# Expert-up tiles inside the gate-matrix stage, later key products and a final norm by token half, in a fused two-block kernel

## The chip, the cores and the metric

One Trainium2 chip, one core of it. The metric is the device time of one execution in microseconds (us): the median of three runs of the kernel before is 1892.19 us (1892.02 to 1892.68).

## The reference, cut to what matters

Two transformer blocks over 256 tokens of width 1024, one after the other, then a final RMS norm, all in float32. The parts that the change touches are these:

```
# first block, gated delta rule, both directions, 4 heads of 128
A     = where(strict, (k*beta) @ k.T * decay, 0);  t_inv = inverse(A + eye)
W, U  = t_inv @ (k*beta*exp(G)), t_inv @ (v*beta);  state and output by scan
# first block, expert layer (16384 experts, 8 heads, the best 16 of each head per token)
act   = gelu(einsum('td,thkd->thk', h2, u_table[experts]))
y     = einsum('thk,thkd->td', gate * act, v_table[experts])
# second block, feed-forward
u     = causal_dwconv(h @ ffn_up, w, b);  x = x + (gelu(u_gate) * u_val) @ ffn_down
return rms_norm(x, final_norm_g)
```

## The kernel before, in words

Activations lie transposed (features on the partitions, 256 tokens along the free axis). Weights come as one stream of tiles of 128x1024 float32 (512 KB) through a ring of four slots, loaded by SP in order; a slot is loaded again when its tile has been used (`tiles_done`, or `w_lo` where the tile is split). Each engine's program is written out by hand in order; semaphores tie them together.

**Split products.** Most weight tiles are cut into a high part (ScalarE copies to `fp32r`, L1330, L1311) and a low part (VectorE or GpSimd subtracts, L2085, L2008, L2494, L2339). A product is then three `fp32r` passes in place of one float32 product (`PASSES`, L151): an up tile (`experts_up`, L816) is 24 matmuls of 256 columns, a down tile (`experts_down`, L827) 12 of 512. Plain float32 products with whole tiles exist too: `full` (L756) does one tile as 8 products of 256 columns; the trace shows each float32 product as two matmul instructions.

**The expert layer.** There is no gather: all 16384 experts are computed, 128 tiles up and 128 down, and the result is weighted by a gate matrix that is zero but for the chosen ones. `NU` = 48 up tiles run first, while VectorE routes (top 16 of 16); their gelu goes to `Wa` (L1345). Then the gate stage (L851 to L861): for each of 32 groups of 8 tokens, VectorE builds one-hot matrices `hot1` (L2069, L2074) and `hot2` (L2071), ScalarE scales seven slices of `hot1` (L1362), TensorE does 8 float32 products of 128 columns (L860) into one of three pairs of PSUM banks, ScalarE takes the columns from `NU` on out to `Wb` (L1357) and VectorE multiplies the first `NU` into `Wa` (`w_gate`, L2064, behind `hot2` of two groups later). Then 48 down tiles with what is in `Wa` (L864 to L868), and then 80 pairs of one up and one down tile (L869 to L876), each up tile's gelu being gated with `Wb` (L1392, L2101).

**The delta rule.** Four steps `n`; in each, six levels `l` of a blockwise inverse for both directions `d`. Per level TensorE does `level_products` (L595: products, then a transpose of `z`), VectorE masks the products (L1903), TensorE does `level_update` (L612), VectorE subtracts (L1910). Other work is laid between: `tok_turn` (L553, transposes of keys and values by token, moved out by ScalarE at L1240), `key_products` of the next step (L572, behind `level_update` of level 2, waiting on `gaps` that VectorE writes in `gap_rows`, L1818), POOL's products, and on VectorE `mod_tail` (L1809), 32 row sums over 1024 columns of streamed tiles: four before the levels, one or two behind each level. `in_tile(38)` is the last input projection.

**The end.** `ffn_up` and `ffn_down` (L1022, L1040) over 22 blocks; per block ScalarE and VectorE norm, convolve, gate and split the activations. The last `ffn_down` waits for all of it for all 256 tokens; then ScalarE squares the four PSUM banks (L1619), VectorE adds the sums, ScalarE takes the root (L1621), VectorE scales the four banks (L2427), and SP writes them out.

## Time and profile before

| | |
|---|---|
| runs | 1892.02, 1892.19, 1892.68 us |
| profiled execution | 1892.63 us |
| its span, first to last instruction | 1890.6 us |
| mean granted TensorE clock | 0.986 |
| busy share: TensorE, VectorE, ScalarE, GpSimd | 96%, 66%, 53%, 8% |
| delta-rule stage | about 250 to 437 us |
| gate stage | about 682 to 778 us |
| 48 down tiles; 80 up/down pairs | 778 to 911 us; 911 to 1360 us |
| end, from the last `ffn_down` on | 1878 to 1890.6 us |

Times are microseconds from the start of the span unless marked ns. A busy share is an average over stages with different limits. Instructions are named by the line of the kernel that issues them. Idle time of TensorE is named with the instruction that ended it.

### The profile page before, as it was taken

The numbers are of one execution on the slowest core, as the hardware profiler recorded it, in microseconds if no ns is written. First come the engines' busy times: TensorE is split into PE (matmuls) and PEld (weight loads), VectorE is DVE, ScalarE is ACT, GpSimd is POOL, SyncE is SP. The second block draws the span as 40 slices with busy tenths as digits, with TensorE's granted clock in tenths as the row PEclk, the third lists the DMA queues.
The fourth block names the chain that finished last, engine by engine and source line by source line (L and its number), as shares of the span: only waits on it lengthen the run. The fifth ranks groups of instructions, "written<-read, shape, count | busy, mean of one in ns | idle before, by whom it ended". The sixth has DMA issues, their size and how long they took to land.

```text
span 1890.6 us, 34445 instructions
## 1 busy us (share of the span) xinstructions
PE 1806.4 (96%) x11798; PEld 1620.1 (86%) x11798; DVE 1248.8 (66%) x2494; ACT 1005.2 (53%) x2017; POOL 148.9 (8%) x118
## 2 busy tenths in 40 slices
PE   8999999999999977899999999999899999999997
PEld 2878789898899976788899999999799899889997
DVE  2786465565388979766666666666676766348886
ACT  2545633241146679766555555555557667036665
POOL 0000003330164520000000000000000000000000
PEclk9999989899999999999999999999999999999999
DMA  7523232123455520255555555555454533445553
GB/s 265 192 100 106 85 111 76 62 91 133 143 172 176 177 89 1 73 194 191 193 183 188 188 187 187 182 188 187 145 183 145 175 123 123 150 162 179 188 181 119
DMA packets 77267, 283.28 MB, mean 150 GB/s; under 512 B 8576, under 2 KB 8576, under 8 KB 76928
## 3 DMA queue, kind: packets, MB, share of 16 engines
q1 hardware_dynamic: 77184, 282.16, 44.6%
q8 instruction: 53, 0.87, 0.2%
q14 instruction: 30, 0.25, 0.0%
HBM read 281.08 MB, written 1.05 MB: 149 GB/s over the span
## 4 chain that ended last, share of the span: by engine, by line
PE 83%; DVE 11%; ACT 3%; issue 1%; DMA 1%; POOL 1%; PEld 0%; PEldq 0%; POOLq 0%; SPq 0%; DVEq 0%; ACTq 0%
PE banks L834 19%; PE banks L822 17%; PE banks L433 7%; PE banks L1035 7%; PE banks L896 6%; PE banks L763 5%; PE banks L1047 3%; PE banks L620 2%; PE banks L604 2%; DVE split L2071 2%; DVE arena L2069 2%; PE banks L1008 1%; PE banks L786 1%; PE banks L401 1%; PE banks L609 1%
## 5 line engine op out<-in xcount | busy, mean ns | idle before, releaser
L1330 ACT ACTIVATE split<-arena 128x512 fp32r<-128x512 f32 x508 | 318.9, 629 | 146.7 <-PE banks L822 83.3
L822 PEld LDWEIGHTS banks<-split 128*128 128x128 f32 x3072 | 379.5, 192 | 11.1 <-DVE split L2008 3.1
L822 PE MATMUL banks<-split 128*128 128x256 f32 x3072 | 383.0, 283 | 3.2 <-DVE split L2008 2.3
L834 PE MATMUL banks<-split 128*128 128x512 f32 x1536 | 364.9, 391 | 2.7 <-issue 2.7
L2085 DVE TENSOR_TENSOR split<-arena,split 128x512 fp32r<-128x512 f32 x412 | 281.9, 690 | 117.0 <-ACT split L1330 111.3
L834 PEld LDWEIGHTS banks<-split 128*128 128x128 f32 x1536 | 284.3, 189 | 58.8 <-issue 2.9
L1311 ACT ACTIVATE split<-arena 128x512 fp32r<-128x512 f32 x264 | 164.5, 627 | 106.2 <-PE banks L1035 52.1
L896 PE MATMUL banks<-split 128*128 128x256 f32 x1344 | 169.5, 286 | 4.0 <-DVE split L2160 3.9
L896 PEld LDWEIGHTS banks<-split 128*128 128x128 f32 x1344 | 164.7, 193 | 7.6 <-issue 6.6
L433 PEld LDWEIGHTS banks<-split 128*128 128x128 f32 (+1 forms) x936 | 132.0, 191 | 28.2 <-issue 13.9
L433 PE MATMUL banks<-split 128*128 128x256 f32 (+2 forms) x936 | 150.9, 320 | 4.3 <-DVE split L1652 3.4
L1035 PEld LDWEIGHTS banks<-split 128*128 128x128 f32 x1056 | 129.7, 192 | 1.7
L2137 DVE TENSOR_TENSOR split<-arena,split 128x512 fp32r<-128x512 f32 x128 | 87.3, 690 | 65.8 <-ACT split L1311 64.7
L1035 PE MATMUL banks<-split 128*128 128x256 f32 x1056 | 130.8, 283 | 0.0
L2339 DVE TENSOR_TENSOR split<-arena,split 128x512 fp32r<-128x512 f32 x132 | 89.1, 687 | 14.7 <-ACT split L1311 14.6
L2494 POOL TENSOR_TENSOR split<-arena,split 128x512 fp32r<-128x512 f32 x68 | 90.9, 1364 | 71.8 <-DVE split L2008 51.2
L860 PE MATMUL banks<-split,arena 128*128 128x128 f32 x512 | 66.9, 286 | 28.4 <-DVE arena L2074 28.4
L860 PEld LDWEIGHTS banks<-split,arena 128*128 128x128 f32 x512 | 61.9, 198 | 33.4 <-DVE split L2071 29.3
L763 PE MATMUL banks<-arena 128*128 128x256 f32 x384 | 86.4, 385 | 3.7 <-DVE arena L2334 2.2
L763 PEld LDWEIGHTS banks<-arena 128*128 128x128 f32 x384 | 74.0, 193 | 14.8 <-DVE arena L2334 2.6
L1652 DVE TENSOR_TENSOR split<-arena,split 128x512 fp32r<-128x512 f32 x78 | 52.8, 688 | 43.2 <-ACT split L1096 42.4
L2101 DVE TENSOR_TENSOR arena<-arena 128x256 f32<-128x256 f32 x80 | 49.1, 614 | 45.0 <-ACT arena L1392 44.9
(378 smaller groups left out, 2382.5 us busy)
## 6 DMA issues: line engine op xcount, KB each, us to landing
arena<-wstream SPq DMA_DIRECT2D x525, 512.0 KB, 3.3
arena<-x_t SPq DMA_DIRECT2D x1, 2048.0 KB, 12.9
arena<-matsa SPq DMA_DIRECT2D x1, 1234.0 KB, 6.2
out_t<-arena SPq DMA_DIRECT2D x4, 256.0 KB, 2.1
arena<-mats SPq DMA_DIRECT2D x1, 576.0 KB, 7.9
arena<-crow SPq DMA_DIRECT2D x1, 512.0 KB, 7.0
arena<-rows SPq DMA_DIRECT2D x1, 512.0 KB, 5.6
arena<-mats SPq DMA_DIRECT2D x1, 449.0 KB, 3.9
```

The lines of the kernel that those rows point to most:

```text
L433: mm = pe.matmul(ps[0:rows, b, 0:m], w_parts[:, c, (2 * t + k // 4) % 4, P * (k % 4):P * (k % 4) + rows], hp[:, e, k, 0:m], start=(k == 0 ...
L763: mm = pe.matmul(ps[:, b, 0:S], w[:, P * k:P * k + P], src[:, k, :], start=(k == 0), stop=(k == KT - 1))
L822: mm = pe.matmul(ps[:, 4 + b, 0:S], w_parts[:, c, (2 * m + half) % 4, P * k:P * k + P], h_parts[:, e, 4 * half + k, :], start=(half == 0 a ...
L834: mm = pe.matmul(ps[:, 2 * tt + half, :], g_parts[:, e, j % 2, P * tt:P * tt + P], w_parts[:, c, (2 * m + half) % 4, :], start=(first and ...
L860: pe.matmul(ps[:, W_BANKS[g % 3] + t // 4, P * (t % 4):P * (t % 4) + P], hot1[g % 2][:, t, :], hot2[:, g % 2, t, :].bitcast(F32), start=Tr ...
L896: mm = pe.matmul(out, w_parts[:, c, (2 * m + half) % 4, P * k:P * k + P], src[:, e, 4 * half + k, :], start=(half == 0 and k == 0 and c + ...
L1035: mm = pe.matmul(ps[:, 4 + 2 * (f % 2) + m, 0:S], w_parts[:, c, (2 * (M_FFN + x) + half) % 4, P * k:P * k + P], h_parts[:, e, 4 * half + k ...
L1311: act.activation(w_parts[:, 0, h % 4, :], ring[:, slot, 512 * half:512 * half + 512], ACT.Copy).then_inc(sem["w_hi"], 1)
L1330: act.activation(w_parts[:, 0, (2 * m + half) % 4, :], ring[:, peer_slot(m), 512 * half:512 * half + 512], ACT.Copy).then_inc(sem["w_hi"], 1)
L2085: dve.tensor_tensor(w_parts[:, 1, (2 * m + half) % 4, :], ring[:, slot, 512 * half:512 * half + 512], w_parts[:, 0, (2 * m + half) % 4, :] ...
L2339: dve.tensor_tensor(w_parts[:, 1, h % 4, :], ring[:, tile_of(M_FFN + x) % RING, 512 * half:512 * half + 512], w_parts[:, 0, h % 4, :].bitc ...
L2494: pool.tensor_tensor(w_parts[:, 1, (2 * m + half) % 4, :], ring[:, (N_PEER + m) % RING, 512 * half:512 * half + 512], w_parts[:, 0, (2 * m ...
```

## The change

Eight of the up tiles (48 to 55) are no longer split: as float32 tiles they come in another order of the stream (by chunk of 128 features, each tile holding one chunk for all eight) and are multiplied by `h2` as 64 plain products of 256 columns, accumulated in banks 4 to 7: 8 before the gate stage's first group, 52 spread over the groups (one or two ahead of each), 4 behind the last. The gate stage keeps two pairs of banks in place of three, and `w_gate` stands between `hot1` and `hot2`. Chunks 0 to 3 of `h2` stay in a buffer of their own; VectorE rebuilds chunks 4 to 7 there from the high and low parts. The eight tiles' gelu and gating ride in the down loop, which now runs over 56 tiles; 72 pairs follow.

In the delta rule, four of the eight `tok_turn` go around `in_tile(38)`, the others to levels 2 and 4; `key_products` of the next step go ahead of `level_update` of level 3; the `mod_tail` are spread anew. At the end the last convolution, gate, split, down product, squares, root and scaling go by half of the tokens, and the square root's table is called for ahead.

```diff
+NX = 8
+NT = NU + NX
-        W_BANKS = (0, 2, 6)
+        w_banks = lambda g: ps[:, 2 * (g % 2):2 * (g % 2) + 2, :].rearrange("p b (t j) -> p (b t) j", j=P)
+        plain_out = lambda q: ps[:, 4 + q // 2, S * (q % 2):S * (q % 2) + S]
+        plain_done = lambda g: NX + 52 * g // (S // 8 - 1)
...
+            def plain_products(a, b):
+                for k, q in (divmod(c, NX) for c in range(a, b)):
+                    n = N_PEER + NU + 2 + k
+                    if q == 0:
+                        tile_ready(n)
+                        if k >= 4:
+                            pe.wait_ge(sem["normed"], k - 2)
+                    mm = pe.matmul(plain_out(q), tile_at(n)[:, P * q:P * q + P], h2k[:, k % 4, :], start=(k == 0 and q % 2 == 0),
+                                   stop=(k == KT - 1), skip_group_check=True)
+                    if q % 4 == 3:
+                        mm.then_inc(sem["tiles_done" if q == 7 else "half_used"], 1)
+            plain_products(0, plain_done(0))
             for g in range(S // 8):
+                if g:
+                    plain_products(plain_done(g - 1), plain_done(g))
                 pe.wait_ge(sem["hot2_ready"], g + 1)
-                if g >= 3:
-                    pe.wait_ge(sem["w_gated"], g - 2)
+                if g >= 2:
+                    pe.wait_ge(sem["w_gated"], g - 1)
...
+            plain_products(plain_done(S // 8 - 1), NX * KT)
# ScalarE, down loop
+            def expert_gelu(j, i=0):
+                if j < NT:
+                    out = plain_out(j - NU)
...
+                if j + 2 < NU:
                     done_hi(j + 2, i, step)
-                peer_hi(NU + j + 2, 1, i, step // 4)
+                elif j + 2 < NT:
+                    gated_hi(j + 2)
+                peer_hi(NT + j + 2, 1, i, step // 4)
+                if NU <= j + 4 < NT:
+                    expert_gelu(j + 4)
# VectorE, gate stage
+            def plain_used(k):
+                dve.wait_ge(sem["tiles_done"], N_PEER + NU + k + 1)
+                dve.sem_inc(sem["w_lo"], 2)
+                if k < 4:
+                    dve.tensor_tensor(h2k[:, k, :], h_parts[:, 0, 4 + k, :].bitcast(F32), h_parts[:, 1, 4 + k, :].bitcast(F32),
+                                      ALU.add).then_inc(sem["normed"], 1)
...
+                if g >= 2:
+                    w_gate(g - 2)
                 dve.tensor_tensor(hot2[:, g % 2, :, :], ...).then_inc(sem["hot2_ready"], 1)
...
-                if g >= 2:
-                    w_gate(g - 2)
+                for k in range(KT):
+                    if g >= 2 and plain_done(g - 3 if g > 2 else -99) < NX * (k + 1) <= plain_done(g - 2):
+                        plain_used(k)
# delta rule, TensorE
             key_products(0, 1)
+            tok_turn(0)
+            tok_turn(1)
             in_tile(38)
+            tok_turn(2)
+            tok_turn(3)
...
-                    if n == 0 and l < 5:
-                        tok_turn(2 * l - 2)
-                        tok_turn(2 * l - 1)
+                    if n == 0 and l in (2, 4):
+                        tok_turn(2 + l)
+                        tok_turn(3 + l)
...
+                    if n < 3 and l == 3:
+                        for d in range(2):
+                            key_products(n + 1, d)
                     for d in range(2):
                         level_update(n, l, d)
...
-                            if l == 2:
-                                key_products(n + 1, d)
# delta rule, VectorE
-            for q in range(2):
-                mod_tail(next(tails))
+            TAILS = ((2, 1, 1, 1, 2, 3), (1, 0, 1, 0, 2, 2), (1, 1, 0, 0, 2, 2), (1, 1, 1, 1, 2, 2))
-                    for q in range(2 if (n, l) in ((0, 1), (0, 2), (3, 4), (3, 5)) else 1):
+                    for q in range(TAILS[n][l - 1]):
                         mod_tail(next(tails))
# the end, TensorE
+            def last_down():
+                f, x = FT - 1, 3 * FT - 1
+                for tt in range(2):
+                    pe.wait_ge(sem["g_lo"], P + f + tt + 1)
+                    for half in range(2):
+                        pe.wait_ge(sem["w_lo"], 2 * (M_FFN + x) + half + 1)
+                        for c, e in PASSES:
+                            mm = pe.matmul(ps[:, 2 * tt + half, :], ...)
+                        mm.then_inc(sem["bank_final"], 1)
# the end, ScalarE
+            last_parts()
+            act.activation(small[:, 84:85], eps, ACT.Sqrt)
...
+            for tt in range(2):
+                final_square(2 * tt)
+                link(final_square(2 * tt + 1))
+                final_root(tt)
# the end, VectorE
+            last_taps(0)
+            last_gate(0)
+            last_taps(1)
+            last_gate(1)
+            for tt in range(2):
+                last_lo(tt)
+            for tt in range(2):
+                dve.wait_ge(sem["final_root"], tt + 1)
+                link(dve.reciprocal(vec[:, 62 + tt:63 + tt], vec[:, 60 + tt:61 + tt]))
+                for b in range(2 * tt, 2 * tt + 2):
+                    dve.scalar_tensor_tensor(outb[:, b, :], ps[:, b, :], vec[:, 62 + tt:63 + tt], ...)
```

## Rows read from the trace of the kernel before

**Rows 1.** The page: shares of the chain that ended last, by engine and line.
```profile
PE 83%; DVE 11%; ACT 3%; issue 1%; DMA 1%; POOL 1%; PEld 0%; PEldq 0%; POOLq 0%; SPq 0%; DVEq 0%; ACTq 0%
PE banks L834 19%; PE banks L822 17%; PE banks L433 7%; PE banks L1035 7%; PE banks L896 6%; PE banks L763 5%; PE banks L1047 3%; PE banks L620 2%; PE banks L604 2%; DVE split L2071 2%; DVE arena L2069 2%; PE banks L1008 1%; PE banks L786 1%; PE banks L401 1%; PE banks L609 1%
```
**Rows 2.** The chain in time, down loop and pairs: start us, length us, what.
```profile
778.38 132.31 PE banks L834 x576
...
941.67 2.87 PE banks L822 x24
944.54 2.75 PE banks L834 x12
```
**Rows 3.** The chain in time, eight plain float32 tiles.
```profile
468.55 27.89 PE banks L763 x128
```
**Rows 4.** The chain in time, gate stage: first group, one middle group, last group.
```profile
684.31 3.77 PE banks L860 x16
...
719.64 1.00 DVE arena L2069
720.64 1.14 DVE split L2071
721.77 0.26 DVE arena L2074
722.03 0.47 DVE arena L2064
...
773.63 2.04 PE banks L860 x16
```
**Rows 5.** Timeline, a middle group: start, us, engine, line, instruction, [idle before].
```profile
722.17 2.02 PE L860 MATMUL banks<-split,arena 128*128 128x128 f32 x16 [0.84 <-DVE arena L2074]
...
723.53 2.16 ACT L1362 ACTIVATE arena<-arena 128x128 f32<-128x128 f32 x7
```
**Rows 6.** Windows: us, then busy of PE, PEld, DVE, ACT, POOL, clock, DMA, GB/s.
```profile
259.00:274.20 15.20, 15.18 (x108) 14.97 (x108) 8.57 (x17) 4.56 (x8) 0.82 (x1) 0.78 0.49 166
684.30:690.00 5.70, 5.69 (x29) 5.70 (x30) 4.16 (x5) 4.35 (x14) 0.00 (x0) 0.56 0.00 1
703.00:740.00 37.00, 26.13 (x209) 24.04 (x208) 37.00 (x53) 35.49 (x105) 0.00 (x0) 1.00 0.01 1
```
**Rows 7.** The chain in time, delta rule: level 1 products and a full-clock x16 group.
```profile
262.44 1.60 PE banks L604 x8
...
269.03 0.84 PE banks L604 x8
...
328.03 1.79 PE banks L584 x16
```
**Rows 8.** Timeline, delta rule: key products with the idle before them, one tail.
```profile
275.78 3.31 PE L577 MATMUL banks<-arena 128*128 128x128 f32 x16 [1.57 <-DVE arena L1823]
...
317.35 3.64 PE L577 MATMUL banks<-arena 128*128 128x128 f32 x16 [2.04 <-DVE arena L1826]
...
318.73 1.22 DVE L1813 SCALAR_TENSOR_TENSOR arena<-arena 128x1024 f32<-128x1024 f32 x1
...
362.41 3.78 PE L577 MATMUL banks<-arena 128*128 128x128 f32 x16 [2.04 <-DVE arena L1826]
```
**Rows 9.** Waits, delta rule, 249.8 to 440: who for whom, total us, times, longest.
```profile
PE banks L620 <- DVE arena L1903: 3.4, 5, 1.4
```
**Rows 10.** The chain in time, the end.
```profile
1878.05 3.04 PE banks L1047 x12
...
1881.10 2.42 ACT arena L1619 x8
...
1883.55 1.28 ACT L1621
1884.83 0.32 ACTq L78
...
1885.37 0.75 DVE arena L2427
```

More of the change, by code:

```diff
@@ L235, in build @@
         rT = top("rT", 3, S)
+        h2k = top("h2k", 4, S)
         h2T = buf("h2T", KT, S)
+        h2 = lambda k, n=1: (h2k if k < 4 else h2T)[:, k % 4:k % 4 + n, :]
         yT = buf("yT", KT, S)
@@ L605, in level_products @@
                 mm.then_inc(sem["y_done"], 1)
-                if l == 1 and n:
-                    pe.wait_ge(sem["wu_ready"], step_at(n - 1, d))
+                if l == 1:
+                    if n:
+                        pe.wait_ge(sem["wu_ready"], step_at(n - 1, d))
+                    else:
+                        pe.wait_ge(sem["tok_ready"], 3 + d)
                 for h in range(4):
@@ L1047, in ffn_down @@
                             mm = pe.matmul(ps[:, 2 * tt + half, :], g_parts[:, e, f % 2, P * tt:P * tt + P],
-                                           w_parts[:, c, (2 * (M_FFN + x) + half) % 4, :], start=False, stop=(last and c == 1),
+                                           w_parts[:, c, (2 * (M_FFN + x) + half) % 4, :], start=False, stop=False,
                                            skip_group_check=True)
@@ L1370, in done_hi, with gated_hi, down_step @@
                     sem["g_hi"], 1)
[L1372 to L1379 removed]
+            def expert_gelu(j, i=0):
+                if j < NT:
+                    out = plain_out(j - NU)
+                else:
+                    used(2 * j - 1 if j > NT else 2 * NT, 1, i, 4)
+                    out = ps[:, 4 + j % 2, 0:S]
+                act.activation(gelu[:, j % 2, :], out, ACT.Gelu_apprx_tanh).then_inc(sem["gelu_done"], 1)
+            def gated_hi(j, i=0):
+                act.wait_ge(sem["gated"], 2 * i + j - NU + 1)
+                act.activation(g_parts[:, 0, j % 2, :], gated[:, j % 2, :], ACT.Copy).then_inc(sem["g_hi"], 1)
+            def down_step(j, i=0, step=0):
+                used(NT + j, 0, i, step)
+                peer_hi(NT + j + 2, 0, i, step // 4)
+                used(NT + j, 1, i, step)
+                if j + 2 < NU:
+                    done_hi(j + 2, i, step)
+                elif j + 2 < NT:
[3 more added lines that the diff above has]
+                    expert_gelu(j + 4)
             act.wait_ge(sem["w_gated"], S // 8)
@@ L1386, in _ @@
                     down_step(j, i, 4)
-            for j in range(NU - 4, NU):
-                down_step(j, last=(j >= NU - 2))
-            def expert_gelu(j, i=0):
-                used(2 * j - 1 if j > NU else 2 * NU, 1, i, 4)
-                act.activation(gelu[:, j % 2, :], ps[:, 4 + j % 2, 0:S], ACT.Gelu_apprx_tanh).then_inc(sem["gelu_done"], 1)
-            def gated_hi(j, i=0):
-                act.wait_ge(sem["gated"], 2 * i + j - NU + 1)
-                act.activation(g_parts[:, 0, j % 2, :], gated[:, j % 2, :], ACT.Copy).then_inc(sem["g_hi"], 1)
+            for j in range(NU - 4, NT):
+                down_step(j)
             def step(j, i=0, last=False):
@@ L1593, in ff_step @@
                 ahead(x + 1, 1, i4)
-                up_out(f, 1, i4)
-                ff_gelu(f, i4)
-                used(x + 2, 0, i4)
-                ahead(x + 2, 0, i4)
-                used(x + 2, 1, i4)
-                ahead(x + 2, 1, i4)
+                if f < FT - 1:
+                    up_out(f, 1, i4)
+                    ff_gelu(f, i4)
+                else:
+                    ff_gelu(f)
+                    last_up_out()
+                if f < FT - 1:
+                    used(x + 2, 0, i4)
+                    ahead(x + 2, 0, i4)
+                    used(x + 2, 1, i4)
+                    ahead(x + 2, 1, i4)
             for x in range(2):
@@ L2091, in done_lo @@
                                   g_parts[:, 0, j % 2, :].bitcast(F32), ALU.subtract).then_inc(sem["g_lo"], 1)
-            def down_step(j, i=0, step=0, last=False):
-                tile_lo(NU + j + 2, 0, i, step // 4)
-                if not last:
-                    done_lo(j + 2, i, step)
-                tile_lo(NU + j + 2, 1, i, step // 4)
             def gate(j, i=0):
@@ L2107, in gated_lo, with down_step @@
                     sem["g_lo"], 1)
+            def down_step(j, i=0, step=0):
+                tile_lo(NT + j + 2, 0, i, step // 4)
+                if j + 2 < NU:
+                    done_lo(j + 2, i, step)
+                elif j + 2 < NT:
+                    gated_lo(j + 2)
+                tile_lo(NT + j + 2, 1, i, step // 4)
+                if NU <= j + 3 < NT:
+                    gate(j + 3)
             def step(j, i=0, last=False):
@@ L2122, in _ @@
                     down_step(j, i, 4)
-            for j in range(NU - 4, NU):
-                down_step(j, last=(j >= NU - 2))
-            tile_lo(2 * NU + 2, 0)
-            gate(NU)
-            gated_lo(NU)
-            with dve.Fori(0, (P - 2 - NU) // 2) as i:
-                for j in (NU + 1, NU + 2):
+            for j in range(NU - 4, NT):
+                down_step(j)
+            tile_lo(2 * NT + 2, 0)
+            gate(NT)
+            gated_lo(NT)
+            with dve.Fori(0, (P - 2 - NT) // 2) as i:
+                for j in (NT + 1, NT + 2):
                     step(j, i)
```

145 lines of the change are left out of this document (90 added, 55 removed).

## The prediction

> **What bounds the kernel now.** I read the page's chain first: TensorE holds 83% of the path that ended last, VectorE 11%, ScalarE 3% [rows 1]. So most of the time is a row of matmuls, and what a removed matmul is worth depends on whether its stage is in the 83 or in the 11. The chain in order of time tells that. In the expert layer's down loop and pair loop nothing but TensorE stands in it: 48 down tiles in 132.3 us, that is 2.76 each, and each up tile 2.87 [rows 2]. In the gate stage it is the reverse: the middle group is VectorE from end to end, 1.00 + 1.14 + 0.26 + 0.47 = 2.87 us per group of 8 tokens [rows 4], and TensorE works 2.02 of it and then idles 0.84 [rows 5]. The windows say the same of 703 to 740 us: VectorE busy 37.00 of 37.00, ScalarE 35.49, TensorE 26.13 at full clock [rows 6]. Thus a down or up tile costs its full price, and TensorE work of up to 0.84 us per group should be free. In the delta rule I read the timeline for idle in front of `key_products` [rows 8] and the waits for VectorE's masks [rows 9]; at the end of the kernel everything is serial [rows 10].
>
> **Part by part.** The sum is made against the profiled execution, 1892.63 us (span 1890.6 and 2.0 around it), 0.44 above the median.
>
> *1. Eight up tiles leave the pair loop.* 8 x 2.87 [rows 2] = -23.0. The down tiles stay 128 in number. Eight down steps get a gelu and a gating beside them; TensorE's 2.76 per step covers them, since ScalarE and VectorE do the same gelu and gating beside two tiles' splits in the pair loop without appearing in its chain. Splits of these eight tiles fall away too, at no gain, being hidden already. Should the cover fail, eight steps would each lose some tenths: 0 to +4, taken 0.
>
> *2. The plain products.* A whole tile of 8 such products took 27.89 / 8 = 3.49 us, or 0.436 each [rows 3]; 64 take 27.9. Of these 52 lie over 31 groups: 21 groups get two, 10 get one. A group is then 2.02 + 0.87 = 2.89 or 2.02 + 0.44 = 2.46 on TensorE, on average 2.75, against VectorE's 2.87: it fits with 0.12 to spare, and a group of two runs over by 0.02, given back by the next of one. VectorE asks for TensorE's results only two groups later, so this overrun reaches nobody. Price 0.
>
> The 8 products ahead of the first group do lie on the path. VectorE's first three instructions (1.00 + 1.14 + 0.26 with starts) end just before the first product at 684.31 [rows 4], so the stage opens some 2.6 us earlier, at 681.7. At full clock 8 x 0.436 = 3.5 end at 685.2, 0.9 late; but then the first group, which now takes 3.77 at half clock, would take 2.04 [rows 4]: -0.8 in all. At half clock, which stood after this same gap (0.56 granted in 684 to 690 [rows 6]), they take 7.0, to 688.7: +4.4. The third `hot1` waits for that group. I take +1.5.
>
> The last 4 products, 1.7 us, run while ScalarE takes out and VectorE gates the last group. Price 0. The tiles come by DMA in a stage that moves almost nothing (0.01 DMA share [rows 6]); the first four slots are free as early as now.
>
> *3. VectorE and the order in the gate stage.* Four sums of 256 columns that rebuild `h2`; the trace's 384-column operation takes 0.47 [rows 4], so 0 to +1.9, taken +1.4. On VectorE each is ahead of the next `hot1`. `w_gate` ahead of `hot2` costs nothing itself, but it now wants ScalarE's copy of two groups before right after `hot1`. ScalarE needs 2.16 for seven slices [rows 5] and the copy behind them; at 35.49 of 37.00 busy [rows 6] its copy ends just about when `hot1` does. Queued behind that wait are `hot2`, the last slice and the next `hot1`. A lag of 0 to 0.1 in 31 groups is 0 to +3; I take +0.5. The third pair of banks is not missed: with two, TensorE waits for a gate that now comes 1.4 us earlier in VectorE's order.
>
> Gate stage together: 1.5 + 1.4 + 0.5 = +3.4 (from -0.8 to +9.3).
>
> *4. Delta rule, key products.* Now TensorE reaches them before VectorE has written the gaps: it idles 1.57, 2.04 and 2.04, then does the 16 instructions in 3.31, 3.64 and 3.78 [rows 8], where a same-shaped set takes 1.79 at full clock [rows 7]. Idle 5.65 and excess 5.36, and after the third the next products are still at half clock, 1.60 for 0.84 [rows 7], some 1.7 in all. Behind the products of level 3, they find the gaps written; what stays is VectorE's own course (gap rows, a `mod_tail` of 1.22 [rows 8], masks) which is late next in steps 0 and 1. -12.7 + about 1.7 of that = -11 (-5.6, if only the idle goes and the clock still drops, to -12.7).
>
> *5. `tok_turn`.* Two go ahead of `in_tile(38)` and two behind it, where TensorE idles for the first masks; level 1 and level 3 of step 0 lose two each, about 0.9 at full clock and 1.5 at half. The stretch 259 to 274 ran at 0.78 although TensorE was busy 15.18 of 15.20 [rows 6]: it had idled before, and level 1's products took 1.60 where later 0.84 [rows 7]. With the turns in the gap most of that goes. At best 0.22 x 15.2 = 3.3 of clock and 0.9 of moved work, at worst the turns delay the masks by as much as they save: 0 to -4.2. I take -2.5.
>
> The Trainium skill (TensorE: Matmul & The Clock Gate, Part 4: PE-mode transpose) says that transposes do not count as activity for the gate, which speaks against this: turns put in the gap would not raise the clock. By that rule -2.5 becomes about -1. No row separates it, since turns here always run among products.
>
> *6. `mod_tail` spread.* TensorE waited 3.4 us in five places for the mask that stands behind tails [rows 9]; the new table empties levels 2 and 4 of step 1 and levels 3 and 4 of step 2 and fills levels 5 and 6, where TensorE has the mask turn or `apply_inverse` to do. Worth 2.3 of idle and about 1.0 of clock after it: -3.3 (0 to -4.5; three tails behind level 6 of step 0 beside GpSimd could cost +1).
>
> Delta rule together: -11 - 2.5 - 3.3 = -16.8.
>
> *7. The end.* Now, after the last product at 1881.1: squares 2.42, table 1.28, root 0.32, reciprocal 0.2, four scalings of 0.68 = 2.7, then the write [rows 10]. Half the tokens reach TensorE some 0.5 earlier. The table load moves beside the last products and ends near 1879.1, so the first two squares end at 1880.3, the second two at 1882.2 with the first root (0.65 with its sum) between, the second root at 1882.8, reciprocal and two scalings at 1884.4. The present order ends at 1888.1: -3.7 (-2.5 to -4.5).
>
> The Trainium skill (ScalarE: Activation LUTs, What ACT_TABLE_LOAD costs) gives about 2.66 us for a switch with its drain; the row shows 1.28 and the root directly behind. By the page the end would gain 1.4 more; the row decides.
>
> **Sum:** -23.0 + 3.4 - 16.8 - 3.7 = -40.1: 1852.5 profiled, 1852 as a median.
>
> **Rivals.**
> *A, the gate stage gives more back.* TensorE's margin is 0.12 per group. If a plain product mixed among small ones costs 0.55 rather than 0.436, the average is 2.94, and with a ScalarE lag of 0.2 per group the stage grows by 6 to 9 on top: 1861. For it: ScalarE and VectorE have no slack either [rows 6]. Against: L763 gives 0.436 with its loads hidden [rows 3].
>
> *B, the delta rule keeps its time.* VectorE becomes the next bound at level 3, or the clock drops anyway. Then only the idle of 5.65 in part 4 goes, and little else: -7 in place of -16.8: 1862. For it: after such idle the clock stayed down for several us [rows 7, 8]. Against: the chain there is TensorE in nearly every piece.
>
> *C, slower than before.* TensorE at half clock for the whole gate stage: 2 x 2.75 = 5.5 per group, 31 x (5.5 - 2.87) = +82, to 1934. It decides from where TensorE's group passes 2.87 + 40.1 / 31 = 4.2, a granted clock under 0.65. For it: 0.56 at the stage's start [rows 6]. Against: 1.00 from 703 on with a lighter load than the new one.
>
> *D, the change does less than it says:* plain products that wait for tiles, or a down loop bound by its new gelu work. It would be seen as 5 to 10 us, 1860.
>
> **How the numbers follow.** Forecast 0.68, A 0.12, B 0.12, D 0.05, C 0.02, and 0.01 for no difference. The forecast's own range is 1845 to 1858. A, B and D end at 1860 to 1862; for 8 in 10 I give 1842 to 1864. A measurement of this kernel tells some 0.2% (4 us) from no change: faster 0.97, same 0.01, slower 0.02.
>
> **What would show it.** Pair loop: 72 pairs at 5.62 each. Gate stage: period 2.87 to 2.90, TensorE busy about 2.75 of it; its first group later than 685 or 688 tells the clock. Delta rule: `key_products` with no idle before them and 1.8 us long, clock at 1.00 where it was 0.78. End: first square near 1879, last scaling near 4 us behind the last product. The forecast is wrong if the gate stage's period passes 3.0, or if idle turns up at the masks of level 3.

## The result and the profile after

The changed kernel takes 1847.45 us (median of 1845.28, 1845.32, 1849.59 and 1849.76), the one before 1892.2 beside it: a ratio of 0.976, 95% interval 0.975 to 0.978. The prediction was 1852, with a range of 1842 to 1864. The profiled execution took 1849.76 us (span 1848.0, mean granted clock 0.990), 42.9 less than before's 1892.63; the predicted sum was 40.1.

The page of the kernel after, shares of the chain by engine and line. L848 is the down tile, L836 the up tile, L890 the gate stage's products, L873 the plain products, L629 `level_update`.
```profile
PE 85%; DVE 9%; ACT 3%; issue 1%; DMA 1%; POOL 1%; PEld 0%; PEldq 0%; POOLq 0%; SPq 0%; DVEq 0%; ACTq 0%
PE banks L848 19%; PE banks L836 16%; PE banks L438 7%; PE banks L927 7%; PE banks L1066 7%; PE banks L777 5%; PE banks L1090 3%; PE banks L629 2%; PE banks L610 2%; DVE split L2165 2%; PE banks L1039 2%; PE banks L800 2%; DVE arena L2161 1%; PE banks L406 1%; PE banks L618 1%
```
TensorE's share went up from 83 to 85% and VectorE's down from 11 to 9% [rows 1]. More than half of what VectorE lost lies in the delta rule, where TensorE no longer waits for it; most of the rest lies in the gate stage.

The stages, from their first instructions in both profiled executions:

| stage | before | after | difference | predicted |
|---|---|---|---|---|
| delta rule, to the next branch's first product | 446.13 | 427.08 | -19.1 | -16.8 |
| gate stage, opening to first down tile | 96.7 | 99.9 | +3.2 | +3.4 |
| all tiles after it, to the last expert product | 581.9 | 557.2 | -24.7 | -23.0 |
| from there to the last `ffn_up` | | | +1.2 | 0 |
| the last `ffn_up` to the end | 22.25 | 18.93 | -3.3 | -3.7 |
| sum | | | -42.7 | -40.1 |

The +1.2 is a stretch in the norm between the blocks, where nothing was changed: the granted clock was 0.59 and 0.56 in 1328 to 1336 us here, and only 0.57 in 1372 to 1376 us before. The profiles of the edited kernels below take between 506.4 and 509.6 us from the last expert product to the last `ffn_up`, with 508.1 before and 509.2 after, so this is scatter. Now the chain of the kernel after in time, gate stage and down loop: start us, length us, what. L2161 and L2168 are `hot1`, L2165 is `hot2`, L2156 `w_gate`, L2151 a sum of `h2`.
```profile
662.76 5.41 PE banks L873 x16
668.17 1.80 PE banks L890 x16
669.99 0.78 DVE arena L2161
...
672.95 0.33 DVE arena L2151
...
757.86 2.02 PE banks L890 x16
759.88 1.73 PE banks L873 x8
761.61 1.01 issue
762.62 152.59 PE banks L848 x672
```
The 8 products ahead took 5.41, the first group 1.80 in place of 3.77 [rows 4]. The last plain products (L873 x8, four products) and the wait behind them fill 2.74, where 2.7 went by without them before. 56 down tiles take 152.59, 2.725 each; the 48 of before took 2.756 [rows 2], because their first ones ran at a lower clock after TensorE had idled (granted 0.57 in 778.4 to 782 us before, 1.00 in 762.6 to 766 us after).

The window of the kernel after that answers to [rows 6] (PE, PEld, DVE, ACT, POOL busy, clock, DMA share, GB/s):
```profile
703.00:740.00 37.00, 34.64 (x248) 29.62 (x247) 37.00 (x52) 34.62 (x102) 0.00 (x0) 1.00 0.10 33
```
TensorE went from 26.13 to 34.64 of 37.00 with VectorE still at 37.00. The group period went from 2.86 to 2.86 and 2.90 in turn, and 3.20 in the four groups that hold a sum.

The timeline of the kernel after in the delta rule, all of TensorE there for one stretch (start, us, engine, line, instruction, [idle before]). L583 is `key_products`.
```profile
275.34 0.61 PE L618 MATMUL banks<-arena 128*128 128x128 f32 x4
275.79 1.95 PE L583 MATMUL banks<-arena 128*128 128x128 f32 x16
277.57 1.90 PE L629 MATMUL banks<-arena 128*128 128x64 f32 x16
279.31 1.06 PE L610 MATMUL banks<-arena 128*128 128x64 f32 x8
```
No idle before the key products, 1.95 in place of 3.31 to 3.78 [rows 8], and 1.06 behind them: full clock. The waits of TensorE from 249 to 427 us, kernel after (us, times, longest):
```profile
PE banks L687 <- ACTq L383: 0.7, 1, 0.7
PE banks L629 <- DVE arena L1988: 0.7, 2, 0.5
PE banks L610 <- DVE arena L1927: 0.3, 1, 0.3
PE banks L653 <- ACT arena L1333: 0.3, 1, 0.3
```
All that is left is 2.0 us, of which 0.7 is for the masks that cost 3.4 [rows 9]. The end of the kernel after, chain in time:
```profile
1838.43 0.31 ACT split L1634
...
1838.76 1.28 ACT L1693
...
1840.05 0.20 ACT arena L1693
1840.25 1.17 ACT arena L1697 x4
...
1842.06 1.16 ACT arena L1697 x4
...
1844.10 0.75 DVE arena L2555
```
The table (L1693) is called for 0.02 behind ScalarE's last split and stays in the chain; the first square (L1697) starts 1.5 us before TensorE's last product ends at 1841.7.

### The profile page after: what moved, and what is told of

Same layout as the page of the kernel before. It is cut to its first block, busy times and chain, and to the rows that moved or that the text cites. A ratio compares the mean times of both kernels' runs of the same rounds, so it can differ in the third digit from the quotient of the medians.

```text
span 1848.0 us, 34175 instructions
## 1 busy us (share of the span) xinstructions
PE 1799.8 (97%) x11734; PEld 1608.6 (87%) x11734; DVE 1238.3 (67%) x2486; ACT 996.3 (54%) x2007; POOL 147.0 (8%) x118
## 4 chain that ended last, share of the span: by engine, by line
PE 85%; DVE 9%; ACT 3%; issue 1%; DMA 1%; POOL 1%; PEld 0%; PEldq 0%; POOLq 0%; SPq 0%; DVEq 0%; ACTq 0%
PE banks L848 19%; PE banks L836 16%; PE banks L438 7%; PE banks L927 7%; PE banks L1066 7%; PE banks L777 5%; PE banks L1090 3%; PE banks L629 2%; PE banks L610 2%; DVE split L2165 2%; PE banks L1039 2%; PE banks L800 2%; DVE arena L2161 1%; PE banks L406 1%; PE banks L618 1%
## 5 line engine op out<-in xcount | busy, mean ns | idle before, releaser
L1377 ACT ACTIVATE split<-arena 128x512 fp32r<-128x512 f32 x492 | 309.0, 629 | 134.9 <-PE banks L836 76.8
L836 PEld LDWEIGHTS banks<-split 128*128 128x128 f32 x2880 | 355.4, 192 | 10.5 <-DVE split L2093 3.1
L848 PE MATMUL banks<-split 128*128 128x512 f32 x1536 | 361.9, 390 | 1.0 <-issue 1.0
L836 PE MATMUL banks<-split 128*128 128x256 f32 x2880 | 358.7, 283 | 3.2 <-DVE split L2093 2.3
L2183 DVE TENSOR_TENSOR split<-arena,split 128x512 fp32r<-128x512 f32 x396 | 270.8, 690 | 105.5 <-ACT split L1377 99.6
L848 PEld LDWEIGHTS banks<-split 128*128 128x128 f32 x1536 | 283.8, 188 | 57.3 <-issue 1.4
L1358 ACT ACTIVATE split<-arena 128x512 fp32r<-128x512 f32 x264 | 164.5, 627 | 108.9 <-PE banks L1066 52.3
L927 PE MATMUL banks<-split 128*128 128x256 f32 x1344 | 171.5, 289 | 3.9 <-DVE split L2262 3.9
L927 PEld LDWEIGHTS banks<-split 128*128 128x128 f32 x1344 | 167.1, 196 | 7.3 <-issue 6.9
L2239 DVE TENSOR_TENSOR split<-arena,split 128x512 fp32r<-128x512 f32 x128 | 87.3, 690 | 68.6 <-ACT split L1358 67.5
L1066 PEld LDWEIGHTS banks<-split 128*128 128x128 f32 x1056 | 129.7, 192 | 1.7
L1066 PE MATMUL banks<-split 128*128 128x256 f32 x1056 | 130.8, 283 | 0.0
L2441 DVE TENSOR_TENSOR split<-arena,split 128x512 fp32r<-128x512 f32 x132 | 89.1, 687 | 15.4 <-ACT split L1358 15.4
L1738 DVE TENSOR_TENSOR split<-arena,split 128x512 fp32r<-128x512 f32 x78 | 52.8, 688 | 43.2 <-ACT split L1139 42.5
L890 PEld LDWEIGHTS banks<-split,arena 128*128 128x128 f32 x512 | 59.7, 191 | 16.2 <-DVE split L2165 16.1
L1410 ACT ACTIVATE arena<-arena 128x128 f32<-128x128 f32 x224 | 69.0, 389 | 7.7 <-DVE arena L2161 6.0
```

What stands on the lines that cost most here:

```text
L836: mm = pe.matmul(ps[:, 4 + b, 0:S], w_parts[:, c, (2 * m + half) % 4, P * k:P * k + P], h_parts[:, e, 4 * half + k, :], start=(half == 0 a ...
L848: mm = pe.matmul(ps[:, 2 * tt + half, :], g_parts[:, e, j % 2, P * tt:P * tt + P], w_parts[:, c, (2 * m + half) % 4, :], start=(first and ...
L927: mm = pe.matmul(out, w_parts[:, c, (2 * m + half) % 4, P * k:P * k + P], src[:, e, 4 * half + k, :], start=(half == 0 and k == 0 and c + ...
L1066: mm = pe.matmul(ps[:, 4 + 2 * (f % 2) + m, 0:S], w_parts[:, c, (2 * (M_FFN + x) + half) % 4, P * k:P * k + P], h_parts[:, e, 4 * half + k ...
L1358: act.activation(w_parts[:, 0, h % 4, :], ring[:, slot, 512 * half:512 * half + 512], ACT.Copy).then_inc(sem["w_hi"], 1)
L1377: act.activation(w_parts[:, 0, (2 * m + half) % 4, :], ring[:, peer_slot(m), 512 * half:512 * half + 512], ACT.Copy).then_inc(sem["w_hi"], 1)
```

## The experiments

Each is the changed kernel with one edit unless said otherwise. Times are medians; ratios are to the kernel before run beside each, with their 95% interval. The first four go against 1847.45, the rest against the changed kernel run again, 1845.47; the last four were run apart from it. Within the delta rule I measure from the start of the first instruction of `level_update` to the start of its last one, and call it the span of the updates: 163.7 before, 145.5 after. In the gate stage, "the groups" is the time from the first `hot1` that waits for TensorE to the first down tile: 90.3 before, 92.6 after.

**Key products back.**
```diff
-                    if n < 3 and l == 3:
-                        for d in range(2):
-                            key_products(n + 1, d)
                     for d in range(2):
                         level_update(n, l, d)
+                            if l == 2:
+                                key_products(n + 1, d)
```


> The changed kernel with key_products put back behind level_update of level 2; all else as changed. Theory (TensorE idles for the gap rows, and the granted clock falls after each idle): the three places grow by what the two traces differ there, 4.3 + 3.5 + 5.1 = 12.9 us, to about 1860; the trace shows idle of 1.5 to 2 us ahead of each of the three key_products groups and the 16 instructions of each at half clock, 3.3 to 3.8 us. Rival (the clock has nothing to do with it, only the idle counts): +5.7, to 1853, with the groups at 1.8 us each. Rival (tok_turn and the tails made the gain): +0 to +2.

1862.2 us, 0.984 (0.982 to 0.986): 14.8 slower. The updates span 159.9, 14.4 more. Timeline of this kernel:
```profile
272.16 2.79 PE L583 MATMUL banks<-arena 128*128 128x128 f32 x16 [1.57 <-DVE arena L1908]
274.74 1.81 PE L610 MATMUL banks<-arena 128*128 128x64 f32 x8
```
Its waits for the gaps are 6.0 in all (1.6 and 4.4); the other 8.4 is mostly the half clock behind them (1.81 for the 1.06 above). The granted clock was 0.50 in 315 to 320 us and 0.55 in 355 to 360 us, where the changed kernel has 1.00 from the first update to the last. The rival that only the idle counts (5.7) falls, and so does the one that the turns and tails made the gain.

**Delta rule alone**: the kernel before with the three edits of the delta rule.
```diff
 # before.py
+            tok_turn(0); tok_turn(1)      # and two behind in_tile(38)
+                    if n < 3 and l == 3:  # key_products ahead of level_update
+            TAILS = ((2, 1, 1, 1, 2, 3), (1, 0, 1, 0, 2, 2), (1, 1, 0, 0, 2, 2), (1, 1, 1, 1, 2, 2))
```


> The kernel before with the delta-rule edits alone (tok_turn, key_products, mod_tail spread); expert layer and end as before. Theory: the stage is worth what the traces differ there, 18.9, so 1873.3 (2 either way, by where the clock stands at the stage's start). Rival (part of it is given back behind, since the last tails are later and the branch tiles with them): 1876 to 1880, with waits for tiles in the branch products behind the stage.

1871.47, 0.988 (0.987 to 0.990): -21.3. Its updates span 145.6, and from there to the gate stage's first product it takes 254.5, where the kernel before takes 254.4. Nothing is given back there. Behind the expert layer its profile is 2.0 longer than before's (532.3 for 530.3), though the program is the same; the granted clock was 0.50 in 1350 to 1355 us and 0.64 in 1480 to 1485 us. The rest of the change is then 1871.47 - 1847.45 = 24.0, where the prediction's other parts sum to 23.3.

**A quarter of the plain products.**
```diff
+                    if q % 4 != 3:
+                        continue
                     mm = pe.matmul(plain_out(q), ...)
```


> The changed kernel with 48 of the 64 plain products left out (those of six of the eight tiles; the output lacks them); waits, sums and tiles stay. Theory (the products between the groups ride in TensorE's idle; only those ahead of the first group count): TensorE is busy 20.9 us less in the gate stage, yet the stage is shorter by only 1 to 2.5 us, to 1845 to 1846.5; the period of a group stays 2.87 to 2.89. Rival (they are paid in part, by lag between the engines, and this is the 2.3 us by which the groups grew): the stage is shorter by 4 or more, to 1843.

1846.17, 0.976 (0.974 to 0.977): 1.3 faster, inside the scatter. The groups take 92.60, with all products 92.63. The 52 between the groups cost nothing. With 2 products ahead in place of 8 the first `hot1` that waits comes 6.0 us after the stage opens, where it was 7.2.

**Each plain product twice.**
```diff
+                    pe.matmul(plain_out(q), ..., start=(k == 0 and q % 2 == 0), stop=False)
                     mm = pe.matmul(plain_out(q), ..., start=False, stop=(k == KT - 1))
```


> The changed kernel with each of the 64 plain products issued twice (eight experts tiles then count double in the output). Theory (TensorE is then the bound in the gate stage, period 2.02 + 2 x 0.73 = 3.48 for 2.89 now): +0.59 x 31 = 18.3, +3.5 ahead of the first group, +0.7 behind the last: +22.5, to 1870. Rival (TensorE is the bound already): all 64 x 0.436 = 27.9, to 1875. Rival (there is still slack elsewhere): under +18.

1860.2 (1857.83 to 1861.33), 12.75 slower where the theory said 22.5. The theory falls. Chain of this kernel, one group and the products behind it:
```profile
671.62 1.78 PE banks L892 x16
673.41 0.43 PE banks L873 x2
673.84 0.43 PE banks L875 x2
```
The 16 gate products take 1.78 here, from the start of their first to the start of the product behind them, and not the 2.02 of [rows 5]. The 2.02 runs to the end that the profile gives their last product, and a product that follows directly starts before that end. Timeline of the changed kernel, the last group and the plain products behind it:
```profile
757.86 2.02 PE L890 MATMUL banks<-split,arena 128*128 128x128 f32 x16
759.72 1.89 PE L873 MATMUL banks<-arena 128*128 128x256 f32 x8
```
From start to start that is 1.86. So 0.16 of the 2.02 is the last product's end, which the next one overlaps, and another 0.08 goes when the group doesn't wait. A group here is 1.78 + 104 x 0.431 / 31 = 3.23 on TensorE, and the trace has 3.22 from one `hot1` to the next as the mean of 29 groups. So the slack was 2.87 - 1.78 = 1.09 per group, not the 0.84 that stands as idle. The third rival, slack elsewhere and under +18, holds.

**The changed kernel again**, not edited.

> The changed kernel once more, unaltered. Its four first runs stand at 1845.3 and 1849.7, two each, and the traces of five kernels with the same delta-rule stage differ in where TensorE is granted 1.2 in place of 2.4 GHz at the same place in the program. Theory (the stretches at half clock fall anew in each execution, and this is the scatter): the stages differ between this profile and the first only in such stretches, and time falls as the mean granted clock rises, about 1.8 us for 0.001. Rival (two modes of the DMA or of the engines' starts): the difference sits in a stage at full clock.

1845.47 (1844.89 to 1849.92, five runs). Its profile (span 1843.1, clock 0.993) differs from the first one in a few places only. Chain of this execution:
```profile
659.43 3.72 PE banks L873 x16
663.15 1.80 PE banks L890 x16
```
5.41 became 3.72. From the stage's opening to the first `hot1` that waits it is 5.6 us here, 7.2 in the first execution and 6.4 in the kernel before. The other place is the start of the delta rule, windows first of the first execution, then of this one:
```profile
249.00:255.00 6.00, 5.28 (x27) 5.13 (x26) 3.64 (x9) 2.34 (x8) 0.00 (x0) 0.59 0.25 83
255.00:262.00 7.00, 7.00 (x55) 7.00 (x54) 5.53 (x12) 3.99 (x10) 0.00 (x0) 0.86 0.03 8
```
```profile
249.00:255.00 6.00, 5.44 (x48) 5.37 (x48) 5.35 (x14) 3.23 (x10) 0.00 (x0) 1.00 0.28 88
255.00:262.00 7.00, 6.52 (x57) 6.11 (x56) 5.49 (x10) 4.36 (x11) 3.04 (x4) 1.00 0.14 37
```
The same program idled the same 0.72 us before both; once the clock fell (0.59 granted), once it stayed. The first `level_update` comes at 265.3 and at 262.0: 3.3 us. So the edits at the start are worth 1.0 or 4.3 over before's 266.3, by luck. In the nine other profiles of kernels with the same start it comes between 261.8 and 265.2. Of the five runs the four at a mean clock of 0.993 took 1844.9 to 1846.1, the one at 0.990 took 1849.92, like the first profile (0.990, 1849.76). The two profiled spans differ by 4.9: 3.3 of it is this place and 1.7 the eight products ahead of the gate stage. The theory holds.

**No plain products ahead**: 12 behind the last group instead of 4.
```diff
-        plain_done = lambda g: NX + 52 * g // (S // 8 - 1)
+        plain_done = lambda g: 0 + 52 * g // (S // 8 - 1)
```


> The changed kernel with no plain product ahead of the first group, 52 between the groups as now, and 12 behind the last. Theory (those ahead cost about 1.2 on the path, as the run with a quarter of them showed, and 4 behind are hidden since the last gating takes 2.7 us): the first groups come 1.2 earlier, and 12 x 0.434 = 5.2 behind the last group outlast the 2.7 by 2.5: +1.3 in all, to 1848.7. Rival (the 8 ahead are what keeps the clock up for the first groups, as the prediction weighed it): the first groups run at half clock again, and nothing is won there: +2.5 or more.

1849.16 (1847.6 to 1852.02), 3.7 slower than 1845.47. Chain of this kernel:
```profile
663.59 3.77 PE banks L890 x16
...
757.28 5.18 PE banks L873 x24
762.47 0.83 issue
```
The first group is at 3.77 again, exactly as before [rows 4], and the first `hot1` that waits comes 6.4 us after the stage opens, as before, 0.9 later than with 8 ahead at full clock (and 0.8 earlier than with 8 ahead at the lower one). Behind, 12 products take 5.18, which covers the hand-over but goes 3.3 beyond it. 0.9 + 3.3 = 4.2 by the trace. The theory of +1.3 falls; the rival, that the 8 buy the clock of the first group, holds.

**Sums on GpSimd.**
```diff
-                    dve.tensor_tensor(h2k[:, k, :], ...).then_inc(sem["normed"], 1)
+            for k in range(4):
+                pool.wait_ge(sem["tiles_done"], N_PEER + NU + k + 1)
+                pool.tensor_tensor(h2k[:, k, :], ...).then_inc(sem["normed"], 1)
```


> The changed kernel with the four sums that rebuild h2 done by GpSimd, which is idle in the gate stage, in place of VectorE. Theory (the gate stage is VectorE's, the sums stand on its path with 0.33 each): the stage is shorter by 1.3, to 1846.1. Rival (a GpSimd operation with two inputs slows VectorE's beside it, as a mod_tail beside GpSimd took 2.1 in place of 1.2): less than 0.5 is left of it, or it turns into a loss. Rival (ScalarE is the bound by now, as its copies end with hot1): nothing changes.

1847.69 (1845.46 to 1849.95): nothing won. Chain of this kernel, two groups' `hot1`, the second beside a sum:
```profile
690.91 1.00 DVE arena L2158
...
693.80 1.53 DVE arena L2158
```
Timeline of the same place, and of a sum earlier in the stage:
```profile
693.59 0.80 POOL L2631 TENSOR_TENSOR arena<-split 128x256 f32<-128x256 f32 x1 [12.64 <-PE banks L873]
693.72 1.62 DVE L2158 TENSOR_TENSOR arena<-arena 128x896 f32<-128x896 f32 x1
...
679.58 1.37 POOL L2631 TENSOR_TENSOR arena<-split 128x256 f32<-128x256 f32 x1 [12.77 <-PE banks L873]
```
Two of the four sums started just ahead of a `hot1`; they took 0.76 and 0.80 and stretched it by 0.53 in the chain. One started in the middle of a `hot1`; it took 1.37 itself, left that `hot1` at its usual length, and its group was 0.04 longer. One ran while VectorE stood idle. So two sums cost more than their 0.33 on VectorE and two cost little, and the groups take 92.45 against 92.61. The rival of the slowed neighbour holds.

**A version meant to be better**: 2 products ahead and 6 behind, sums on GpSimd, the table called for between the two halves.
```diff
+        plain_done = lambda g: 2 + 56 * g // (S // 8 - 1)
+                    if tt == 0:
+                        act.activation(small[:, 84:85], eps, ACT.Sqrt)
```


> Three edits on the changed kernel: 2 plain products ahead of the first group, 56 between the groups and 6 behind; the sums on GpSimd; the square root's table called for between the two halves of the last split. Theory: -1 ahead of the groups, 0 for 56 between them (1.78 + 0.78 = 2.56 on a TensorE that does not wait, against 2.87), 0 behind (2.6 us, hidden by 2.7), -1.3 for the sums, -0.6 at the end (first square 0.7 earlier, then paced by TensorE's banks): -2.9, to 1844.5. Rival (ScalarE's copies bound the groups): -1.6. If it is the fastest, it beats both kernels.

1844.39 (1844.04 to 1847.14), 0.975 (0.974 to 0.977): 1.1 below the changed kernel beside it, with overlapping ranges. It is the lowest median of a kernel that computes everything, not a proven gain. Chain of its end:
```profile
1833.29 0.98 PE banks L1078 x3
...
1834.29 0.69 ACT arena L1698 x2
1834.98 0.70 ACT arena L1698 x2
...
1836.33 1.16 ACT arena L1698 x4
```
The table is gone from the chain, and TensorE's first two banks take its place: 12.9 us from the last but one `ffn_down` to the end in place of 13.3. In the gate stage the other two edits won nothing: 98.8 us against 98.2 in the changed kernel beside it. The first `hot1` that waits comes 0.5 later with 2 products ahead, 6 behind outlast the last gating by 0.7, and the groups between are 0.6 shorter. The profile is lower mainly because the norm between the blocks took 508.1 in place of 509.4, by its clock.

**The sums left out.**
```diff
-                    dve.tensor_tensor(h2k[:, k, :], ..., ALU.add).then_inc(sem["normed"], 1)
+                    dve.sem_inc(sem["normed"], 1)
```


> The changed kernel with the four sums that rebuild h2 left out (four chunks of the plain products then use the first four chunks again, so the output is not the reference's). From the first hot1 that waits for TensorE to the first down product the groups take 92.6 us now and 90.3 in the kernel before. Theory (1.3 of the 2.3 are the sums, 1.0 is w_gate behind hot1 waiting for ScalarE's copy, 0.04 every second group): the groups take 91.3, and the time falls by 1.3. Rival (ScalarE bounds the groups, as moving the sums to GpSimd won only 0.2; while VectorE sums, ScalarE catches up): the groups stay at 92.3 or more.

1842.45 (1841.31 to 1849.79), 0.975 (0.972 to 0.978). The groups take 91.34 in place of 92.61: -1.27, close to 4 x 0.33. That is all the edit gave; the profile's norm between the blocks was 1.3 shorter too (508.1 for 509.4), by its clock.

**`w_gate` behind the last slice again.**
```diff
-                if g >= 2:
-                    w_gate(g - 2)
                 dve.tensor_tensor(hot2[:, g % 2, :, :], ...)
...
+                if g >= 2:
+                    w_gate(g - 2)
```


> The changed kernel with w_gate behind hot2 and the last slice, where it stood before; two pairs of banks and all else as changed. Theory (with two pairs TensorE needs the gate of two groups before, which then comes last in VectorE's group, so TensorE starts a group 0.47 later but still has 0.36 to 0.5 of slack with what it does unwaited): the groups are within 1 us of 92.6. Rival (the order is what makes two pairs bearable): TensorE starts each group behind the gate, works 2.75 to 2.9 and VectorE waits: +0.1 to +0.5 per group, 3 to 15 in all.

1848.59 (1847.25 to 1850.16), 0.977 (0.975 to 0.979). The groups take 92.05: -0.6, too small for the medians, where the clock's scatter hides it (0.990 in this profile). The period is 2.86 in every group without a sum; the 2.90 of every second one is gone. The last group's first product starts 3.06 us after the start of its `hot1`, behind `w_gate`; in the changed kernel it is 3.12 and in the kernel before 2.62.

**Turns back**: the eight `tok_turn` at levels 1 to 4 of step 0 as before.
```diff
-            tok_turn(0)
-            tok_turn(1)
             in_tile(38)
-            tok_turn(2)
-            tok_turn(3)
+                    if n == 0 and l < 5:
+                        tok_turn(2 * l - 2)
+                        tok_turn(2 * l - 1)
```


> The changed kernel with all eight tok_turn back among levels 1 to 4. Theory (turns around in_tile(38) lie in TensorE's idle ahead of the masks; at full clock four of them are 1.8 us of TensorE time): from in_tile(38) to the last level update the stage is 1.8 longer, and a half-clock stretch behind the idle, as in the kernel before at 260 to 266, can add up to 2.3: +1.8 to +4. Rival (level 1 and 3 waited for something else, so the turns were free there): under +0.5.

1850.4 (1848.35 to 1854.1), 0.979 (0.977 to 0.981). Timeline of this kernel:
```profile
256.80 0.66 PE L598 MATMUL banks<-arena 128*128 128x128 f32 x4 [0.63 <-DVE arena L1965]
258.85 1.01 PE L598 MATMUL banks<-arena 128*128 128x128 f32 x4 [1.39 <-DVE arena L1965]
259.65 1.80 PE L610 MATMUL banks<-arena 128*128 128x64 f32 x8
```
The masks' idle is 2.0 where the changed kernel has 0.5, and the clock falls behind it. The last instruction of `level_update` starts at 410.8, against 407.6 in the changed kernel's second profile (+3.2, within the theory's +1.8 to +4) and 410.8 in its first, whose clock fell by itself. Of the 3.2, 0.9 lies within the updates (span 146.4) and is the moved work; the 2.4 ahead of them are no more than what the start moves by itself between profiles, so they are seen in the trace and not proved by the time.

**Tails back**: the old places of the `mod_tail`.
```diff
-            TAILS = ((2, 1, 1, 1, 2, 3), (1, 0, 1, 0, 2, 2), (1, 1, 0, 0, 2, 2), (1, 1, 1, 1, 2, 2))
+            TAILS = ((2, 2, 1, 1, 1, 1), (1, 1, 1, 1, 1, 1), (1, 1, 1, 1, 1, 1), (1, 1, 1, 2, 2, 1))
+            for q in range(2):
+                mod_tail(next(tails))
```


> The changed kernel with the 32 mod_tail spread as before (four ahead of the levels, one or two behind each). Theory (the two traces differ by 5.0 at the levels that were emptied: 3.4 us of TensorE's idle for the masks and the clock that falls behind it): +4 to +5, to 1850.5, with waits for the masks behind levels 3 and 4 of steps 1 and 2. Rival (with key_products later, VectorE has room and the tails no longer matter): under +1.5. Rival (the mod_tail behind level 2, which comes ahead of level 3's masks, now is the one that hurts, since TensorE reaches level 3 some 4 us sooner): the idle sits at level 3.

1856.98 (1854.9 to 1863.89), 0.983 (0.980 to 0.985): 11.5 slower, more than twice what was expected. Its waits, and the timeline behind the longest:
```profile
PE banks L629 <- DVE arena L1990: 6.9, 8, 2.3
```
```profile
264.75 2.62 PE L629 MATMUL banks<-arena 128*128 128x64 f32 x16 [2.28 <-DVE arena L1990]
267.16 1.91 PE L575 MATMUL banks<-arena 128*128 128x128 f32 x8
...
279.71 2.00 PE L629 MATMUL banks<-arena 128*128 128x64 f32 x16 [0.85 <-DVE arena L1990]
...
317.42 2.00 PE L629 MATMUL banks<-arena 128*128 128x64 f32 x16 [0.32 <-DVE arena L1990]
```
The same order of tails made TensorE wait 3.4 in five places before [rows 9] and 6.9 in eight here. The five are here again, with the same lengths within 0.02; the three new ones are those shown: 2.28 ahead of the first update, 0.85 and 0.32 ahead of the updates of level 3 in steps 0 and 1, directly behind the key products. The updates span 154.0, +8.5: of it 3.9 is idle, and most of the rest is the granted clock, 0.66 in 265 to 270 us and again in 330 to 335 us. The first update comes 2.8 later than at 262.0.

## Why the prediction was right, point by point

**The tiles (part 1), -23.0: right, -24.7.** 72 pairs at 5.62 each and 56 down tiles at 2.725; the new gelu and gating are covered. The 1.7 more is the down loop's start: TensorE comes from a filled gate stage and is at full clock, so that a down tile is 2.725 and not the 2.756 of before.

**Plain products (part 2).** That the 52 between the groups are free is shown (a quarter of them: 92.60 for 92.63). The stated margin, 0.12 per group, was mis-sized: the 2.02 of a group that is waited for holds 0.24 that it doesn't need when products follow each other. The true margin is 2.87 - 1.78 - 0.73 = 0.36, which speaks against rival A more than the prediction knew. The 8 ahead, +1.5 of a range -0.8 to +4.4: +0.8 and -0.9 in two executions. The lower bound was reached, because its working (3.5 of products, then 2.04 in place of 3.77) is what happens at full clock: 3.72 and 1.80.

**VectorE in the gate stage (part 3), +1.9: +2.4.** Of it 1.3 is the sums (shown by leaving them out) and 0.6 the place of `w_gate` (shown by putting it back). The last 0.5 stands in the traces at the last group: its first product starts 3.12 us after the start of its `hot1` where 2.62 had done, because `w_gate` now comes ahead of it, and with `w_gate` put back still 3.06. That the two pairs of banks make it so there is what the program's order says; no run with three pairs tests it. Rival A's 6 to 9 didn't come.

**Key products (part 4), -11: right in mechanism and size.** Step by step the traces give 4.3, 3.5 and 5.1 at the three places, 12.9; putting them back costs 14.4. The prediction's own count was 12.7, and the 1.7 that it took off for VectorE's course didn't have to be paid. Rival B fell: with the idle gone the clock stayed up.

**`tok_turn` (part 5), -2.5.** -3.2 against the second profile, nothing against the first: within the bounds 0 to -4.2, and decided by whether the clock falls at 249 us. Only the 0.9 within the updates stands clear of the scatter. In the undisturbed execution the turns stood in the gap and the clock stayed at 1.00. The Trainium skill (TensorE: Matmul & The Clock Gate, Part 4: PE-mode transpose) has transposes not count for the gate; these runs don't bear it out, nor test it alone, since the turns shortened the idle as well as filled it (2.0 to 0.5).

**`mod_tail` (part 6), -3.3: mis-sized.** With the key products and the turns at their new places the old tails cost 8.5 within the updates and 2.8 ahead of them. The step that failed is that each edit was priced from the trace of before as if the others had not been made. Before, TensorE stood idle for the gaps at level 3 and had turns to do at level 1; with both gone it comes to the masks sooner and waits for them at just these places (2.28, 0.85 and 0.32 more), and the clock falls behind the first. That VectorE used the 5.65 us of the gaps to catch up is my reading of it; the places fit, and no run tests it alone. All three back together cost 163.7 - 145.5 = 18.2; key products alone 14.4, tails alone 8.5, turns alone 0.9, together 23.8. They overlap by 5.6. Beside the old key products the tails and turns are worth 18.2 - 14.4 = 3.8, which is near the 3.3; the price was right for an order in which it wasn't used.

**The delta rule as a whole, -16.8: -19.1 in the first profile, -21.3 by the kernel with it alone.** Too small by 2 to 4. Within the updates 18.2 came where 15.2 had been summed: key products 12.9 for 11, the tails' share 4.4 for 3.3, and 0.9 for 0.9 of the turns. The start gave 1.0 or 4.3 for the remaining 1.6.

**The end (part 7), -3.7: -3.3.** Last scaling about 4 us behind TensorE's last product, as said. The table took 1.28 again and runs beside the products, as said. The missing 0.4 stands ahead of the first square: ScalarE's last split, behind which the table is called for, ends 9.7 us after the start of the last `ffn_up` where the working had it near 9.5, and the small root that calls for the table takes 0.20 of its own. The half of the tokens that was to reach TensorE 0.5 earlier reached it 0.1 earlier (9.58 for 9.70 us).

**Rivals C and D:** granted clock 1.00 all through 703 to 740; no wait for a tile in the plain products or the down loop.

What brought the total near is that the tiles, the key products and the end hold nearly nine tenths of the gain (40.9 of 47.1) and were each read from rows that show just that piece. The tails' error of some 5 us is hidden in the total, because it overlaps with the key products.

## What to carry to other kernels

Idle in front of TensorE is paid twice here, once as idle and once in the slower products behind it: 6.0 of idle cost 14.4. Free room on an engine that waits in every round can be more than the idle shown: here 1.09 us per group for 0.84, since the busy time of a group that is waited for holds 0.24 that goes when products follow each other. Push work in and measure with double the load to find it. When two edits feed on the same slack of a third engine, price each with the other already made: one removed wait uncovers the next (3.4 us of waits became 6.9).

## What the runs showed of the hardware

- A float32 group of 16 instructions of 128 columns has a busy time of 2.02 us when it is waited for. The product behind it starts 1.86 after its first one, and 1.78 when nothing is waited for.
- The granted clock after the same idle of 0.72 us differs from execution to execution (0.59 and 1.00 in the same 6 us). It makes 3.3 of the 4.9 us between the kernel's own two profiles: 1845 at a mean clock of 0.993, 1850 at 0.990.
- A 256-column sum on GpSimd that started ahead of VectorE's 896-column `hot1` took 0.8 and stretched it from 1.00 to 1.53, more than the sum's 0.33 on VectorE itself; one that started within a `hot1` took 1.37 itself and left it as it was.
